# Sixteen heads as one sequence, sinks as a column of the scores, and the start address of the stationary activations

## The reference, cut to what matters

```python
def mixer_a(x, w_qkv, b_qkv, sinks, w_o, b_o, cos, sin):      # layers 0 and 3
    qkv = x @ w_qkv + b_qkv                                   # 16 query heads, 4 key/value heads of 64
    q, k = apply_rope(q, cos, sin), apply_rope(k, cos, sin)   # first 16 of 64 columns are turned
    o = block_attention(q, k, v, 128, 127, True, sinks)       # window of 128
    return o @ w_o + b_o

def block_attention(...):
    m = max(s.max(-1), sink)
    p = exp(s - m)
    l = p.sum(-1) + exp(sink - m)
    return (p @ v) / l
...
x = layer_norm(DN_ALPHA * x + h, ln_g, ln_b)                  # DN_ALPHA = 8 ** 0.25
```

## Time and profile before

| | us |
|---|---|
| median of three runs | 2531.65 |
| the profiled execution | 2531.4 |
| its span (first to last instruction) | 2529.6 |
| TensorE busy | 2384.8 (94%) |
| VectorE busy | 1509.2 (60%) |
| ScalarE busy | 1259.6 (50%) |
| GpSimd busy | 478.2 (19%) |
| mean granted TensorE clock | 0.976 |

### The profile page before, as it was taken

The page is one execution under the profiler, slowest core; times in us unless marked ns, Lnnn a source line. Parts: engine busy times, 40 slices in busy tenths (PEclk is TensorE's granted clock), DMA queues, the critical chain, the costliest instruction groups (busy, mean ns, idle before and its releaser), DMA issues.

```text
span 2529.6 us, 36826 instructions
## 1 busy us (share of the span) xinstructions
PE 2384.8 (94%) x15344; PEld 2116.6 (84%) x15344; DVE 1509.2 (60%) x2420; ACT 1259.6 (50%) x1808; POOL 478.2 (19%) x368
## 2 busy tenths in 40 slices
PE   7799999999899998999889979988999999899999
PEld 6589978787699777998669969888989998889998
DVE  5464454545745546546465467656676776566776
ACT  4344445455444455444344446555465565454654
POOL 2230041322400333102320000343100013431000
PEclk9799999999999999999889989999999999999999
DMA  6145543343355533555235543434445544344553
GB/s 247 43 174 183 193 159 132 118 149 117 134 200 184 183 133 134 192 183 191 88 109 195 185 158 134 147 124 150 167 181 185 183 163 147 124 150 167 184 183 134
DMA packets 58182, 398.94 MB, mean 158 GB/s; under 512 B 6816, under 2 KB 7072, under 8 KB 11680
## 3 DMA queue, kind: packets, MB, share of 16 engines
q1 hardware_dynamic: 56864, 393.75, 43.0%
q10 hardware_dynamic: 1152, 2.83, 0.3%
HBM read 395.51 MB, written 1.05 MB: 157 GB/s over the span
## 4 chain that ended last, share of the span: by engine, by line
PE 74%; DVE 11%; ACT 7%; issue 5%; POOL 2%; DMA 0%; POOLq 0%; SPq 0%; DVEq 0%; ACTq 0%
PE b L1142 11%; PE b L1144 11%; PE b L1143 11%; PE b L1076 11%; PE b L1077 10%; PE b L1078 10%; PE b L1081 6%; PE b L1085 3%; ACT whi L1441 2%; DVE wlo L1785 2%; ACT S L1438 2%; DVE b L1809 1%; DVE st L1866 1%; DVE b L1864 1%; DVE xl L1816 1%
## 5 line engine op out<-in xcount | busy, mean ns | idle before, releaser
L1785 DVE TENSOR_TENSOR wlo<-raw,whi 128x2048 fp32r<-128x2048 f32 x351 | 826.5, 2360 | 454.9 <-ACT whi L1441 454.0
L1441 ACT ACTIVATE whi<-raw 128x2048 fp32r<-128x2048 f32 x362 | 691.0, 1910 | 358.3 <-PE b L1144 226.3
L1142 PE MATMUL b<-xh,whi 128*128 128x256 f32 x2560 | 724.3, 283 | 4.1 <-DVE wlo L1785 4.1
L1144 PE MATMUL b<-xh,wlo 128*128 128x256 f32 x2560 | 720.0, 281 | 0.0
L1143 PE MATMUL b<-xl,whi 128*128 128x256 f32 x2560 | 720.0, 281 | 0.0
L1142 PEld LDWEIGHTS b<-xh,whi 128*128 128x128 f32 x2560 | 483.5, 189 | 9.2 <-DVE wlo L1785 5.0
L1143 PEld LDWEIGHTS b<-xl,whi 128*128 128x128 f32 x2560 | 483.6, 189 | 1.9
L1144 PEld LDWEIGHTS b<-xh,wlo 128*128 128x128 f32 x2560 | 483.5, 189 | 0.0
L1076 PE MATMUL b<-whi,xh 128*128 128x512 f32 x832 | 345.4, 415 | 32.9 <-DVE xl L1816 16.1
L1077 PE MATMUL b<-wlo,xh 128*128 128x512 f32 x832 | 331.2, 398 | 0.0
L1078 PE MATMUL b<-whi,xl 128*128 128x512 f32 x832 | 330.2, 397 | 0.0
(11 more groups left out here) (228 smaller groups left out, 2801.8 us busy)
## 6 DMA issues: line engine op xcount, KB each, us to landing
raw<-in_w SPq DMA_DIRECT2D x362, 1024.0 KB, 4.8
gt<-in_rows SPq DMA_DIRECT2D x8, 512.0 KB, 4.1
bt<-in_rows SPq DMA_DIRECT2D x8, 512.0 KB, 5.0
abq<-in_rows ACTq DMA_DIRECT2D x2, 768.0 KB, 4.4
x<-in_x SPq DMA_DIRECT2D x1, 1024.0 KB, 6.3
bc<-in_rows SPq DMA_DIRECT2D x4, 256.0 KB, 5.0
out<-x SPq DMA_DIRECT2D x4, 256.0 KB, 2.0
msk<-in_masks SPq DMA_DIRECT2D x1, 768.0 KB, 6.3
```

Of the source, the lines that this page charges most:

```text
L1142: pe.matmul(out, wh[:, k, cs], ah[:, kk, :], start=kk == 0 and s == 0, stop=False, skip_group_check=True)
L1144: last = pe.matmul(out, wl[:, k, cs], ah[:, kk, :], start=False, stop=final and k == 3, skip_group_check=True)
L1441: return ac.activation(out, i, ACT.Copy)
L1785: ve.tensor_tensor(B.wlo[s][:, :], B.raw[r][:, :], B.whi[s][:, :], ALU.subtract).then_inc(sem["loV"], 1)
```

## The change

Four things are edited.

1. A sink mixer has one attention of eight pairs (ten steps) instead of two of four (twelve). Step 4 waits until the second half of the queries is turned. Bias, rotation and turning of q and k follow each token tile at once (`then` in `tok_out`), the rotation runs on VectorE (`rope_v`), keys are doubled as the bias is added, and `k2` is gone. `pace`, `drive(..., 5)` and `drive(..., 6)` stay.
2. The sink is a score column: `S` has pieces of 386 columns, two of them for the sink, written by GpSimd (`fill`); the minimum starts from the sink, and `exp` and its sum cover it. `floor` and `sink` are gone; `heads` comes ahead of `probs` and `exp` of the step.
3. The closing rows begin as soon as block 2 is there. The roundings of the last weights (`hi`, `lo`) and block 2's first rows are emitted ahead of what is left of the attention and ahead of `warm` (the load of the square root's table); while `closing` is set, `pump` emits no `lo`.
4. `xh` and `xl` have 16 spare columns; for x = 0, 2, 4, 6 (the inputs of the four mixers) they are used from column 8 on, 32 bytes further. `scale_gb` is left only ahead of layer 3's mixer; elsewhere `add` multiplies x by DN_ALPHA itself. `scale_x` runs on VectorE, and `abo` is loaded earlier.

```diff
-        for v in range(n + 2):
-            if tail is not None and due:
+            if v % 4 == 0 and v < n:
+                while not ready(a + v // 4):
+                    yield
+            for g in due[:1]:
                 tail(due.pop(0))
...
             if v < n:
-                self.step("score", u, v, mask, kidx, sinks is not None)
                 if sinks is not None:
-                    self.counts("floor", (u, v))
-                    self.step("floor", u, v, sinks + 2 * v)
+                    self.counts("filled", (a, v))
+                    self.step("fill", a, v, sinks + 2 * v)
+                self.step("score", a, v, mask, kidx, None if sinks is None else sinks + 2 * v)
...
+            if v >= 2 and sinks is not None:
+                consume(v - 2)
...
-        for blks in ((0,), (1,), (2, 3)):
...
+        for blk in range(2):
+            while blk not in ready:
                 self.pump()
+            self.drive(self.row_acc(name, layer, (blk,), a, "o", blk == 0), 6)
+        while 2 not in ready:
+            self.pump()
+        end, finish = boundary_of(a, False)
+        def last_ready():
+            while 3 not in ready:
+                yield
+            self.drain()
+            self.step("warm", a)
+        self.drive(self.row_acc(name, layer, (2, 3), a, "o", False, end, last_ready), 6)
...
+        self.drive(self.tok_out(("kv", i), "a_w_qkv", j, 1024, 2 * i, True, None, keys))
+        self.pre.append(turn("k", u0, 1))
...
+            def queries(t, u=u, hh=hh):
+                if not t:
+                    self.flush()
+                self.step("q_bias", u, hh, t)
+                rotate("q", u, t)
+            self.drive(self.tok_out(("q", u), "a_w_qkv", j, 512 * hh, 2 * i, False, None, queries), 5)
+            self.pre.append(turn("q", u, 1))
+            if hh:
+                break
...
+            self.side.append(self.attention(u0, 8, "ma", lambda u: ("q", u) in turned, consume,
+                                            lambda v, k: 2 * (v // 4) + (2 * (v % 4) + k) // 4, 64, 16 * j, tail))
...
-            for k in range(3):
-                last = tr(B.bank[b][:, 128 * k:128 * k + 128], B.S[2 * (p_ % 2) + i][:, 128 * k:128 * k + 128])
+            for k, c in enumerate((0, 129, 257)):
+                last = tr(B.bank[b][:, 128 * k:128 * k + 128], S[:, c:c + 128])
...
-        i = v.mine(ve.tensor_tensor(B.bank[b][:, :], B.bank[b][:, :], B.x[:, t, h], ALU.add))
+        if a in (0, 6):
+            i = v.mine(ve.tensor_tensor(B.bank[b][:, :], B.bank[b][:, :], B.x[:, t, h], ALU.add))
+        else:
+            i = v.mine(ve.scalar_tensor_tensor(out=B.bank[b][:, :], in0=B.x[:, t, h], scalar=ALPHA,
+                                               in1=B.bank[b][:, :], op0=ALU.mult, op1=ALU.add))
...
+    def fill(a, v, at):
+        s = v % 2
+        if v < 2:
+            b, n = use["S", a, v, 0]
+            g.wait_ge(f"full{b}", n + 1)
+        else:
+            g.wait_ge("exp", mark["exp", (a, v - 2, 1)])
+        g.wait_ge("sinks", mark["sinks", mixer_of(a)])
+        to = B.S2[s].rearrange("p (h c) -> p h c", h=2)[:, :, 128:386:257]
+        ge.tensor_copy(to, B.nsink[:, at:at + 2].unsqueeze(2).broadcast_to([128, 2, 2])).then_inc(sem["filled"], 1)
...
-        self.xh, self.xl = sb("xh", [128, 8, 256], F32R), sb("xl", [128, 8, 256], F32R)
+        self.acts = sb("xh", [128, 2064], F32R), sb("xl", [128, 2064], F32R)
...
+    def act(self, x):
+        at = 8 if x in (0, 2, 4, 6) else 0
+        return [a[:, at:at + 2048].rearrange("p (k n) -> p k n", k=8) for a in self.acts]
```

More of the change, by code:

```diff
@@ L181, in __init__ @@
         self.lowtick = 0
+        self.closing = False
         self.low_on = {}
@@ L253, in pump @@
     def pump(self, n=1):
-        if self.lows and not self.late:
+        if self.lows and not self.late and not self.closing:
             self.lowtick += 1
@@ L354, in row_acc @@
                 yield
+            if last_ready and not t:
+                yield from last_ready()
             if t:
@@ L551, in mixer_a, with rotate, keys, turn @@
-        self.pre.append(keys())
+        def rotate(part, u, t):
+            self.counts("rope", ((part, u), t))
+            self.step("rope_v", (part, u), part, t)
+        def keys(t):
+            if not t:
+                self.flush()
+                self.counts("sinks", i)
+                self.step("sinks", i)
+            self.step("kv_in", i, u0, t)
+            rotate("k", u0, t)
+        def turn(part, u, wait):
+            for _ in range(wait):
+                yield
+            self.turn((part, u), part, (part, u))
+            turned.append((part, u))
@@ L565, in mixer_a @@
-            self.pre.append(turned())
-            def heads(u=u, hh=hh, done=done):
-                while not done:
-                    yield
-                def consume(g):
-                    self.counts("stat_v", ("sink", u, g))
-                    self.counts("stat_a", ("sink", u, g))
-                    self.step("sink", u, g, 16 * j + 8 * hh + 2 * g)
-                    self.step("heads", u, g, hh)
-                def tail(g):
-                    self.out_part((i, 2 * hh + g), hh)
-                    ready[2 * hh + g] = True
-                yield from self.attention(u, "ma", consume, lambda h: 2 * hh + h // 4, 64, 16 * j + 8 * hh, tail)
@@ new lines, in tail, with scale_x @@
+            def tail(g):
+                self.out_part((i, g), g // 2)
+                ready[g] = True
+            self.side.append(self.attention(u0, 8, "ma", lambda u: ("q", u) in turned, consume,
+                                            lambda v, k: 2 * (v // 4) + (2 * (v % 4) + k) // 4, 64, 16 * j, tail))
+        self.project("a_w_o", j, i, ready, self.boundary)
+    def scale_x(self):
+        for t in range(2):
+            self.counts("xg", ("start", t))
+        self.step("scale_x")
+        yield
@@ L1904, in sinks, with scale_x @@
         v.wait_ge("ab", 32 * (i // 3 + 1))
-        B.sink_i = v.mine(ve.tensor_scalar(B.nsink[:, :], B.sink[:, :], -1.0, None, ALU.mult))
-    def kv_in(i, u0):
+        ve.tensor_scalar(B.nsink[:, :], B.sink[:, :], -1.0, None, ALU.mult).then_inc(sem["sinks"], 1)
+    def scale_x():
         for t in range(2):
-            b, n = use["tok", ("kv", i), t]
-            v.wait_ge(f"full{b}", n + 1)
+            for q in range(2):
+                b, n = use["turned", 0, t, q]
+                v.wait_ge(f"full{b}", n + 1)
+        v.wait_ge("abo", 16)
+        for t in range(2):
+            ve.scalar_tensor_tensor(out=B.x[:, t, :], in0=B.x[:, t, :], scalar=ALPHA, in1=B.abo[:, :], op0=ALU.mult,
+                                    op1=ALU.add).then_inc(sem["xg"], 1)
```

400 lines of the change are left out of this document (170 added, 230 removed).

## The result

The changed kernel takes 2509.68 us (median of four runs, 2507.60 to 2516.44), the kernel before 2531.91 beside it. The ratio is 0.9916, interval 0.9895 to 0.9936: 22 us faster. I had forecast 56 us, 2475.4, with 2462 to 2503 as the range; the result lies outside it, 7 us above its upper end.

A forecast was written before the change was run, and what follows sets the result against it. TensorE was busy 94% of the span, with waits and a low clock in the two sink mixers. Terms 24 + 25 + 2 + 7 - 1.1 - 0.6 = 56.3 us off 2531.65 gave 2475.4 us, range 2462 to 2503.

The forecast's parts named there:

- Part 4: Token-major streams: a shift of xh by 32 bytes saves 6.6 ns a matmul, 7 us in layers 1 and 2.
- the address does nothing: Rival: the shifted activations bring no gain while the rest holds, about 2484 us; chance 0.10.
- The sink mixers: Layers 3 and 0: one attention of eight pairs with the sink in the scores saves 24 and 25 us.
- Projections: Layer 3's projections grow from 32.0 to 40.5 us because steps 0 to 3 of the attention fit in.
- Wait for the second half: Layer 3, ahead of step 4: bias, rotation and transposes of the later queries hold TensorE for 2.9 us.
- The end: Layer 3, from the attention's steps to the first add: 2.2 us, layer 2's 3.2 less 1 us for warm.
- The measure taken from layer 2: An attention step without sinks takes 5.0 us there at full clock; the sink mixers' steps were forecast near it.
- Part 3: Closing rows of layers 1 and 2: moving warm behind the last rounding saves 1 us each, 2 us together.
- The odd start is dear: Rival: all 336 transposes of S read slowly from odd multiples of 4 bytes; above 2500 us, chance 0.04.
- scalar_tensor_tensor: add takes this form 24 times in six boundaries, at a cost of 0.6 us.
- The chain at 1.2 GHz: Rival: sink mixers' steps stay at some 7 us at the low clock, 16 us a mixer lost, 2507 us; chance 0.17.
- nothing changes in effect: Rival: VectorE, crowded in the last projection group, lets the attention begin no earlier; 3 to 8 us lost, 2481 us.

The follow-up runs named there:

- old_places: The changed kernel with every tile but S, PT and the small ones behind them back at the place of the kernel before; 2503.11 us, ratio 0.9886.
- s_1600: The changed kernel with the score tile at 1600 columns instead of 1552; 2497.16 us, ratio 0.9861.
- part4_alone: The kernel before with only the changed addresses of xh and xl (16 spare columns, used from column 8 for the mixers' inputs); 2526.55 us, ratio 0.9979.
- lo_first: The changed kernel with one waiting rounding (lo) of a sink mixer ahead of the bias of the keys' second token tile and each queries' bias; 2503.29 us.
- pv_first: lo_first with the wait for the queries' second half moved inside step 4, behind block 0's tail and pair 2's pv; 2500.49 us, ratio 0.9873.
- All edits together: lo_first with tiles reordered to suit each stream's distance, pv_first's edit, and one rounding less ahead of the sink mixers' closing rows; 2478.22 us, ratio 0.9789.
- no_closing: old_places with the closing rows as before: blocks 2 and 3 waited for together, attention drained and square root's table loaded ahead of the roundings; 2508.17 us.
- s_pad: The kernel before with the score tile 64 bytes a partition longer, so oh and ol start 64 bytes further on; 2536.42 us, ratio 1.0017.
- x_behind: The kernel before with xh and xl placed right ahead of the weight tiles, a multiple of 8192 bytes from them; 2536.93 us, ratio 1.0015.
- all_64: x_behind with every tile from xh on 64 bytes further, distances unchanged; measured once, 2535.1 us.
- apart_128_256: x_behind with xh and xl 128 bytes short of the 8192-byte distance to the weights, oh and ol 256 bytes beyond it; measured once, 2539.6 us.

## Why the prediction was wrong, point by point

**Part 4, 7 us in layers 1 and 2 and 0.8 in each sink mixer: the step that failed.** "What differs is the tile: `xh` lies 32 bytes past a multiple of 64, `oh` at one. I take the difference as the address's." The tiles differ in their starts, but also in how far they lie from the weights, and it is this that counts: a multiple of 256 bytes gives 226.7 to 227.5 ns, 64, 128 or 224 beside it 232.5 to 233.6, and 96 beside it 231.2 (table and the lines above it). From two rows that differ in two things I took one. Half of the rival "the address does nothing" came true, that the token-major stream keeps its pace.

**The diff's other two lines that move tiles, not counted at all.** The wider `S` (part 2) moved `oh` and `ol` from 0 to 64; rows went from 226.7 to 233.3 ns, and columns to 119.9 in 40 of the 50 streams of 96 that have no wait in them. I had checked which starts became multiples of 64 and not what lay behind the tiles that grew. old_places, which has the paces that my forecast assumed (228.7 in the short blocks, 118.3), prices this at 6.6 us (its interval just meets the changed kernel's; the paces of the streams leave no doubt). s_1600 gives 12.5, since its columns run at 117.8, which no term of mine had; that the difference is the gain of part4_alone (6 us, from columns and rows), lost in the changed kernel, fits, but was not shown apart. The Trainium skill ("TensorE: Matmul & The Clock Gate", section "LDWEIGHTS (loading the stationary operand)"), by which a load has no address in it, was right about the token-major stream by accident: no run bears out that places do nothing.

**The sink mixers, 24 and 25 us: mechanism right, terms mis-sized, 13.3 and 16.8 us measured.** For layer 3 term by term, from the timeline: projections 47.6 us for my 40.5; from there to the first pv of step 4, 4.3 for 2.9 (whose own terms, 0.69 + 4 x 0.2 + 1.2, make 2.7); steps 4 to 9, 35.7 for 34; to the add 5.0 for 2.2. Together 92.6 for 79.6.
- *Projections.* I looked at what the later attention adds there and not at what the new position of the bias does to the roundings queued behind it. `keys` is called ahead of the pump that emits `lo`. It costs 4.36 us of waiting, 1.23 us once more for the next tile, and 3.4 x (1 - 0.52) = 1.6 us by the low clock. lo_first shows it: the first wait shrinks to 1.5, the other and the low clock go.
- *Wait for the second half.* I had counted the rotation and not the rounding of 2.28 us that stands ahead of it on VectorE, at 1231.51. And I let TensorE go on at full clock behind the gap. It ran 5.9 us at 0.50; in pv_first, where rows fill the gap, the stage has 0.98.
- *The end.* Two roundings ahead of the first add instead of one; taking one away gave 0.4 us in layer 3, since block 3's own weights then bind.

The measure taken from layer 2 was right: steps of 4.9 us once the clock is up, for 5.0 forecast. All edits together bring the stage to 84.7 us, 21 us under the kernel before. What is left to 79.6 (waits of 2.65 us ahead of the first `out_part`, 1.41 ahead of the last pair's transposes and 1.50 ahead of block 3's rows) was not tried.

**Part 3, 1 us each in layers 1 and 2 and in the mixers' sums.** Nothing in layers 1 and 2 (no_closing: 0.0 and 0.1), 1.5 and 2.0 in the sink mixers. Layer 2's +5.1 us I don't put down to the change: its mixer takes 132.7 to 138.1 us in the kernels measured here, 3.1 us apart even between the kernel before and s_pad, which have the same program. It goes with the granted clock (0.95 over the stage in the changed kernel, 0.99 before, 1.00 in s_1600). All these traces have the same three waits of about 2.3, 1.6 and 2.0 us there; in the kernel before TensorE fell to 1.2 GHz at the last of them alone, in the changed kernel at all three, in s_1600 at none. With half of those stretches taken off, the stage is 131.3 us in the kernel before and in the changed one. What lowers the clock in one execution and not in another stays open.

**The rivals.** *The odd start is dear* fell: the 336 transposes of `S` have a mean of 301 ns in both kernels, and within a group their starts follow at 109.8 ns, 110.0 before. *scalar_tensor_tensor* costs nothing: 689 ns for 686, in the groups by form of the changed kernel. My terms of -1.1 and -0.6 us were both nothing.

```profile
L1101 PE MATMUL b<-cst,S 128*128 128x128 f32 x336 | 53.9, 301 | 9.3 <-DVE ol L2067 8.5 <-ACT S L1453 0.7
...
L1882 DVE SCALAR_TENSOR_TENSOR b<-x,b 128x512 f32<-128x512 f32 x24 | 16.5, 689 | 2.2 <-PE b L1094 2.2
...
L1880 DVE TENSOR_TENSOR b<-b,x 128x512 f32<-128x512 f32 x8 | 5.5, 686 | 0.0
```

*The chain at 1.2 GHz* gave the nearest number (2507), by luck, and is not what happened: of its steps of 7 us there are two, one of 8.7 us behind the gap and the last, of 6.9, with a wait of 1.83 us in it; the others take 4.4 to 5.7, apart from the one that holds the wait for the queries. Of *nothing changes in effect* the remark was right that VectorE is crowded in the last group.

**The balance.** Forecast 56 us, measured 22: 34 are missing, and 36 with the two losses of 1.7 us that never came. The sink mixers gave 30.1 us for 49, so 19 are theirs; 7 are the token-major gain of layers 1 and 2, 2 are part 3 there, and 6.6 the rows and columns that the wider `S` slowed (old_places), of which about 1 lies in the sink mixers and stands twice. That makes some 34. The sum mixes profiled stages with medians, whose gains differ (15.0 and 22.2 us, with layer 2's 5.1 in the first), so the 2 us that it lacks mean nothing. Of the sink mixers' 19, single edits gave back 6.4 (lo_first) and 2.8 (pv_first) in the median; the 2.8 is not clear of noise by itself.

## What to carry to other kernels

When a diff makes a tile larger, list the start of every tile behind it, before and after, and compare the pace of each stream (distance of two starts, not duration) in both traces; a place that suits a tile as the stationary operand can be the wrong one for it as the moving operand. When follow-up work moves closer to its producer in an in-order queue, ask which urgent, ready instruction now stands behind its wait. And a gap of 2 us in front of a dense engine is priced with what the clock does behind it, as a range: in one trace nothing, in the next several us at half speed behind the same wait. Compare stages of two profiles only with their time at 1.2 GHz beside them.

## What the runs showed of the hardware that was not expected

- A long stream of 128x512 float32 matmuls takes 226.7 to 227.5 ns each where stationary and moving tile lie a multiple of 256 bytes apart in the partition, 232.5 to 233.6 ns at 64, 128 or 224 bytes beside it, and 231.2 at 96. The tiles' own starts don't count: moved by 64 bytes together, the fast streams stay fast (x_behind against all_64).
- With the weights stationary and 256 columns moving it is the other way round: 120.0 ns at a distance of 0, 117.8 at 64, 118.3 at 224. At 128 it is 119.9 in 48 of the 50 streams of 96 and 118.7 in those two and in nearly all of another length (apart_128_256).
- At 96 the same columns ran at 119.9 in 40 of 50 streams of the changed kernel and at 117.8 in the other ten, always at one pace through a whole part, in the streams of 155 and 288 ahead of them at 117.8, and at 117.8 to 117.9 throughout where the rows between them lay at 0 (s_1600, part4_alone). That the pace of one stream carries over to the next fits this; it was not tested by itself.
- Behind the same wait of 2.3 us, in the same place of layer 2's mixer, TensorE went on at full clock in one execution (the kernel before) and at 0.51 in another (the changed kernel).
